# First shift and scale computed on TensorE in four column blocks, and the input projection summed block by block

## What is computed

```python
mod = jax.nn.silu(c) @ ada_w + ada_b              # (1, 1024) @ (1024, 6144)
sh_m, sc_m, g_m, sh_f, sc_f, g_f = jnp.split(mod, 6, axis=-1)
h = modulate(rms_norm(x, mix_norm_w), sh_m, sc_m) # xn * (1 + scale) + shift, (256, 1024)
proj = h @ w_in                                   # (1024, 3336)
y_r = rwkv7_group(proj[..., :1792], ...)          # chunks 0 to 6 of 256 columns
y_m = mlstm_group(proj[..., 1792:], ...)          # chunks 7 to 12, and 8 gate columns
```

## Time and profile before

| | us |
|---|---|
| median of 3 runs | 1258.65 |
| lowest, highest | 1250.43, 1260.34 |
| the profiled execution | 1263.12 |
| its span in the profile | 1261.0 |
| mean granted clock of TensorE over the span | 0.914 of full speed |

### The profile page before, as it was taken

How to read it: one execution, slowest core, us unless ns; L and a number is a source line. 1 busy time by engine, 2 the same in 40 slices (tenths; PEclk the granted TensorE clock), 3 DMA queues, 4 the chain that set the end, 5 groups by cost and what they waited for, 6 DMA issues and landing times.

```text
span 1261.0 us, 16196 instructions
## 1 busy us (share of the span) xinstructions
PE 1074.6 (85%) x6588; PEld 817.6 (65%) x6588; DVE 638.4 (51%) x812; ACT 351.5 (28%) x440; POOL 170.9 (14%) x224
## 2 busy tenths in 40 slices
PE   1699987999978889989639795979999976999994
PEld 1578853997535555555218674858888865888883
DVE  4556658546444323323046727375757467553433
ACT  0122014341111111111023104165445215543530
POOL 5400113000100133321020004011111130000000
PEclk9999967999977999999769896779999977999998
DMA  9897728204679999998979603057676461545510
GB/s 344 245 303 252 263 93 332 102 1 168 221 283 409 402 401 356 363 351 319 409 250 369 249 3 131 1 180 264 224 294 237 134 241 76 187 147 195 221 67 34
DMA packets 117162, 287.48 MB, mean 228 GB/s; under 512 B 19398, under 2 KB 45278, under 8 KB 117098
## 3 DMA queue, kind: packets, MB, share of 16 engines
q1 hardware_dynamic: 94514, 245.45, 52.1%
q10 hardware_dynamic: 11032, 27.33, 6.3%
q0 software_dynamic: 11552, 13.79, 3.6%
HBM read 334.23 MB, written 2.62 MB: 267 GB/s over the span
## 4 chain that ended last, share of the span: by engine, by line
PE 67%; DMA 14%; DVE 10%; SPq 3%; ACT 2%; ACTq 2%; issue 2%; POOL 1%; DVEq 0%; POOLq 0%
PE ps L573 29%; DMA arena<-in_moe_w_down_dram 6%; PE ps L2249 4%; PE ps L2584 4%; PE ps L2563 4%; PE ps L2423 3%; DMA ring<-in_w_in_dram 3%; DMA macc<-in_ada_w_dram 3%; PE ps L2611 3%; PE ps L2251 2%; PE ps L2510 2%; PE ps L2689 2%; SPq L763 1%; PE ps L1210 1%; SPq L619 1%
## 5 line engine op out<-in xcount | busy, mean ns | idle before, releaser
L578 DVE TENSOR_TENSOR ring_parts<-ring,arena_parts 128x2048 fp32r<-128x2048 f32 x65 | 146.6, 2285 | 49.8 <-ACT arena_parts L1098 43.2
L573 PE MATMUL ps<-arena_parts,macc_parts 128*128 128x512 f32 x512 | 165.9, 396 | 0.0
L573 PE MATMUL ps<-arena_parts,gate_parts 128*128 128x512 f32 x288 | 115.4, 401 | 8.0 <-DVE hT_parts L578 8.0
L573 PE MATMUL ps<-ring_parts,gate_parts 128*128 128x512 f32 x288 | 114.3, 397 | 0.0
L573 PE MATMUL ps<-arena_parts,hT_parts 128*128 128x512 f32 x288 | 114.2, 397 | 0.0
L573 PEld LDWEIGHTS ps<-arena_parts,macc_parts 128*128 128x128 f32 x512 | 96.2, 188 | 19.5
L573 PE MATMUL ps<-ring_parts,macc_parts 128*128 128x512 f32 x256 | 99.8, 390 | 0.0
L1098 ACT CAST arena_parts<-ring 128x2048 fp32r<-128x2048 f32 x32 | 60.4, 1908 | 86.2 <-DMA ring<-in_mlp_w_dram 44.1
L573 PEld LDWEIGHTS ps<-arena_parts,gate_parts 128*128 128x128 f32 x288 | 55.6, 193 | 20.3 <-DVE hT_parts L578 8.8
L2249 PE MATMUL ps<-hT,ring 128*128 128x256 f32 x288 | 68.0, 400 | 0.0
L2584 PE MATMUL ps<-ring,hT 128*32 128x256 f32 x1024 | 61.6, 394 | 4.2 <-DMA ring<-in_moe_w_gate_dram 2.7
(11 more groups left out here) (529 smaller groups left out, 1826.0 us busy)
## 6 DMA issues: line engine op xcount, KB each, us to landing
ring<-in_mlp_w_dram SPq DMA_DIRECT2D x40, 1024.0 KB, 7.6
arena<-in_moe_w_down_dram SPq DMA_DIRECT2D x16, 2048.0 KB, 12.3
ring<-in_ada_w_dram SPq DMA_DIRECT2D x29, 1024.0 KB, 9.0
ring<-in_mlp_w_dram ACTq DMA_DIRECT2D x24, 1024.0 KB, 7.1
ring<-in_moe_w_up_dram SPq DMA_DIRECT2D x10, 2048.0 KB, 18.5
ring<-in_moe_w_gate_dram SPq DMA_DIRECT2D x10, 2048.0 KB, 16.2
arena<-in_ada_w_dram SPq DMA_DIRECT2D x15, 1024.0 KB, 7.0
ring<-in_w_in_dram SPq DMA_DIRECT2D x13, 1024.0 KB, 12.3
```

Of the source, the lines that this page charges most:

```text
L573: ins = nc.tensor.matmul(o, l, r, start=start and i == 0, stop=stop and i == 2, skip_group_check=True)
L578: return eng.tensor_tensor(lo, x, hi.bitcast(F32), ALU.subtract)
```

## The change

- The matrices for shift and scale no longer go through DVE. They come as eight parts of 1 MB: for each block `b` of 256 output columns one part of shift and one of scale, 1024 x 256 each, in runs of 1 KB, into four homes of their own. SP issues them among the first chunks: parts 0 and 1, chunks 7 and 8, parts 2 and 3, chunks 9 and 10, parts 4 to 7, then chunk 11, ada 8, chunk 12, ada 9, ada 10, chunk 0, and so on. Parts 4 and 5 wait for the product of block 0, parts 6 and 7 for that of block 1.
- PE multiplies `c`, broadcast to 32 columns, by a part (16 products of 256 columns for a block, in four 32-row groups of the output), ACT copies the row out of PSUM, and four products of one column bring it into columns and sum the four groups. DVE adds the biases. DVE and ACT then scale one feature tile each in `hT`, in place; the plain transposed input has been copied there before.
- The four early chunks 7 to 10 have PSUM banks 6, 7, 2, 3 and are summed in pieces: after block `b` its two feature tiles are multiplied (chunks 9 and 10 join at block 1 with four tiles).
- Chunks 11 and 12 come directly after the gate columns, before the mLSTM products; before, they stood among them.
- The features are assigned to tiles in another order (`(t p)` where it was `(p t)`), so the transposes read without a stride.
- All small loads go from ACT to POOL. The product for the bias rows moves behind the gate columns on PE, and its copy and the write of `bias_rows` behind the gate activations on ACT.
- DVE uses ada slots 8 to 23 only; slot 9 moves from before the convolution to behind it.

The core of the diff:

```diff
-        stream = [("ada", n) for n in range(8)]
-        for i, n in enumerate(win_order):
-            stream += [("win", n)] + [("ada", 8 + i)]
-        stream += [("ada", n) for n in range(21, 24)]
+        win_early = win_order[:4]
+        stream = [("win", n) for n in win_early]
+        for n, adas in ((11, (8,)), (12, (9, 10)), (0, (11, 12)), (1, (13, 14)), (2, (15, 16)), (3, (17,)), (4, (18,)),
+                        (5, (19,)), (6, (20, 21, 22, 23))):
+            stream += [("win", n)] + [("ada", i) for i in adas]
...
             for i, (kind, n) in enumerate(stream):
+                if i in (0, 2):
+                    mix_part(i)
+                    mix_part(i + 1)
+                if i == 4:
+                    for j in range(4, 8):
+                        mix_part(j)
                 if i >= RING:
...
-            act.wait_ge(t_bias, 1)
-            nc.scalar.copy(ebc, ps[0:SWA_H, 4, 0:384]).then_inc(a_bias, 1)
-            act.wait_ge(a_bias, 1)
-            act.dma_start(scratch_d.rearrange("h (q l) -> h q l", q=P), ebc.unsqueeze(1).to_broadcast([SWA_H, P, 384])
-                          ).then_inc(bias_out, 16)
             act.wait_ge(x_in, 16)
-            a_norm(act, "n", mod_c[:, 0, :], mod_c[:, 1, :])
...
+            for b in range(4):
+                act.wait_ge(t["n"], STEP[f"n.rows{b}"])
+                c.link(nc.scalar.copy(mix_row, ps[:, 4, :]))
+                c.at(f"n.row{b}")
+                act.wait_ge(v["n"], STEP[f"n.mod{b}"])
+                c.link(nc.scalar.activation(hT[:, 2 * b, :], hT[:, 2 * b, :], ACT.Identity,
+                                            bias=mod_c[:, 0, 2 * b:2 * b + 1], scale=mod_c[:, 1, 2 * b:2 * b + 1]))
+                c.at(f"n.a{b}")
...
             cm.at("m.lf")
-            columns(9)
+            act.wait_ge(t_bias, 1)
+            nc.scalar.copy(ebc, ps[0:SWA_H, 4, 0:384]).then_inc(a_bias, 1)
+            act.wait_ge(a_bias, 1)
+            act.dma_start(scratch_d.rearrange("h (q l) -> h q l", q=P), ebc.unsqueeze(1).to_broadcast([SWA_H, P, 384])
+                          ).then_inc(bias_out, 16)
+            columns(11)
...
+            def mix_rows(b):
+                if b:
+                    pe.wait_ge(a["n"], STEP[f"n.row{b - 1}"])
+                for vec in range(2):
+                    j = 2 * b + vec
+                    pe.wait_ge(mix_in[j % 4], 16 * (j // 4 + 1))
+                    for k in range(KT):
+                        quad = slice(32 * (k % 4), 32 * (k % 4) + 32)
+                        ins = nc.tensor.matmul(ps[quad, 4, 256 * vec:256 * vec + 256], c1_b[:, k, :], mix_home[j % 4][:, k, :],
+                                               start=k < 4, stop=k >= 4, skip_group_check=True)
+                n_.mark(ins)
+                n_.at(f"n.rows{b}")
+                pe.wait_ge(a["n"], STEP[f"n.row{b}"])
+                pe.wait_ge(v["n"], STEP["n.mixc"] if b == 0 else STEP[f"n.mod{b - 1}"])
+                for i in range(4):
+                    ins = nc.tensor.matmul(ps[:, 5, 64 + i:65 + i], mix_row[:, P * i:P * i + P], quad_one, start=True, stop=True)
+                n_.mark(ins)
+                n_.at(f"n.cols{b}")
...
+            for b in range(4):
+                mix_rows(b)
+                for n in win_early[:2] if b < 2 else win_early:
+                    win_part(n, (2 * b, 2 * b + 1))
+                if b == 1:
+                    pe.wait_ge(prm_in, 16 * 14)
+                    nc.tensor.transpose(ps[:, 0, 256:312], prm[0:56, :], ident[0:56, 0:56])
+                    c.mark(nc.tensor.transpose(ps[:, 0, 312:408], prm2[0:96, :], ident[0:96, 0:96]))
+                    c.at("w.prm")
+                    for n in win_early[2:]:
+                        win_part(n, (0, 1, 2, 3))
```

More of the change, by code:

```diff
@@ L266, in program @@
         w_slot = small[:, 60:62]
+        quad_one = small[:, 62:63]
+        c1_b = macc[:, 1, 0:256].rearrange("p (k n) -> p k n", k=8)
+        mix_row = macc[:, 1, 256:768]
+        mix_home = [area(kb, SLOT).rearrange("p (t n) -> p t n", t=8) for kb in (0, 66, 22, 78)]
         third_gu = (0, 8, 40, 16)
@@ new lines, in _ @@
+            c = Counter(act, a["n"])
+            for tt in range(TT):
+                a_square(c, "n", tt)
+            for b in (1, 3):
+                act.wait_ge(t["n"], b + 1)
+                c.link(nc.scalar.copy(hT[:, 2 * b:2 * b + 2, :], ps[:, b, :].rearrange("p (k t) -> p k t", k=2)))
+                c.at(f"n.ev{b}")
+            for b in range(4):
[6 more added lines that the diff above has]
+                c.at(f"n.a{b}")
@@ L1306, in columns @@
                 c.at(f"w.col{n}")
-            for n in (7, 8):
+            for n in win_early:
                 columns(n)
@@ L1331, in _ @@
             cm.at("m.exp")
-            columns(12)
             for n in range(7):
@@ L1606, in _ @@
-            v_norm(dve, "n", mod_c[:, 0, :], mod_c[:, 1, :], mod_mix, meanwhile=lambda: ada_slot(6))
+            c.link(nc.vector.tensor_copy(c1_b, ccol[:, 0:8].unsqueeze(2).to_broadcast([P, 8, 32])))
+            dve.wait_ge(g["c"], STEP["c.ident"])
+            c.link(nc.vector.tensor_reduce(quad_one, ident[:, 0:P:32], AX_X, ALU.add))
+            c = Counter(dve, v["n"])
+            for tt in range(TT):
+                v_mean(dve, c, "n", tt)
+            for tt in range(TT):
+                v_xn(dve, c, "n", tt)
@@ new lines, in win_part @@
+            def win_part(n, ks):
+                loaded(pe, ("win", n))
+                pe.wait_ge(a["n"], STEP[f"n.a{ks[-1] // 2}"])
+                pe.wait_ge(v["n"], STEP[f"n.v{ks[-1] // 2}"])
+                w = slot(("win", n)).rearrange("p (t n) -> p t n", t=8)
+                for j in range(2):
+                    o = win_bank(n)[:, 256 * j:256 * j + 256]
+                    for k in ks:
+                        l, r = ((w[:, k, P * j:P * j + P], hT[:, k, :]) if n < 9 else (hT[:, k, P * j:P * j + P], w[:, k, :]))
+                        ins = nc.tensor.matmul(o, l, r, start=j == 0 and k == 0, stop=k == KT - 1, skip_group_check=True)
+                if ks[-1] == KT - 1:
+                    ins.then_inc(t_win, 1)
@@ L2267, in _ @@
             c.at("w.if")
-            for n in (9, 10):
+            pe.wait_ge(hot_in, 32)
+            nc.tensor.matmul(ps[0:SWA_H, 4, 0:384], rel_sb[0:33, :], hots[0:33, :], start=True, stop=True).then_inc(t_bias, 1)
+            for n in (11, 12):
                 columns(n)
@@ L2283, in _ @@
             m.at("m.sc0")
-            columns(11)
+            columns(0)
             pe.wait_ge(v["m"], STEP["m.z"])
@@ L2288, in _ @@
             m.at("m.sc1")
-            columns(12)
-            columns(0)
+            columns(1)
+            columns(2)
             pe.wait_ge(v["m"], STEP["m.pt"])
@@ L2302, in _ @@
             m.at("m.num")
-            for n in range(1, 6):
+            for n in range(3, 6):
                 columns(n)
```

148 lines of the change are left out of this document (82 added, 66 removed), and 7 rows, old and new, of the table STEP.

## The result

The changed kernel is slower: a median of 1266.87 us against 1258.4 for the kernel before beside it, 20 runs each, a ratio of 1.0079 with a 95% interval of 1.0055 to 1.0102. The medians lie 8.5 us apart, and the ratio is worth 9.9 (7 to 13), where 3 less were forecast: the sign was wrong. That 1266.87 lies within the forecast range of 1243 to 1268 says little, as the range holds both signs. One run of the changed kernel took 3722.39 us; the ratio leaves it out, and the median without it is 1266.42. The profiled execution took 1268.72 us (before 1263.12), its span is 1267.0, the mean granted clock 0.912 (0.914).

The account below looks back on a forecast made before the run. Loads bound the kernel up to 49.85 us, PE afterwards. E 70.7 plus 96.9 put chunk 6's end at 167.6 against 170.65, 3 us less: 1260.1 for the profiled execution, 1255.7 for the median, range 1243 to 1268.

Parts of the forecast that it names:

- packet for packet: Bias write beside ring loads: each engine alternates their packets, so a chunk's load takes 15.4 us, an ada slot's 3.8.
- a stall of 8 us: PE before chunk 2, behind the early chunks: waits 8 us for its load, held up by the bias write.
- the price of a lull: PE's clock after the short chains of blocks 1 to 3: 0 to 2 us each, taken as 1.
- Block plan and loads: First stage: 3.6 us a load, last part at 50; block 1's last row products 29.6; no load waits from block 2.
- The 45 by the Trainium skill's rule of line rate: First-stage loads: if 1 KB runs cost nothing, the last lands at 45 and the stage ends some 3 us sooner.
- E: End of early chunks 7 to 10 on PE, before the gate columns: forecast 70.7 us, low 64.7, high 76.
- The rival of the clock: First stage: PE's clock stays down in the pieces, E 87, chunk 6 at 184, 13 us more, 1272; chance 0.13.
- the sum behind E: PE work from gate columns through chunks 0 and 1: chunk 2 due at E + 36, only 0.7 us added.
- The write: Bias rows on ACT's queue behind the gate activations: eight engines, E + 10.5 to E + 40.5, chunk 2 landing at E + 44.
- Cold start: PE after the stall before chunk 2: the lower clock adds 1 us.
- From there on: Chunk 2 to chunk 6: DVE's shifts and slots nearly late, last column sum and chunk 6 taken as 9 us.
- The sum to chunk 6: End of chunk 6 on PE: E + 96.9 = 167.6 against 170.65 before, 3 us less.

Follow-up runs that it names:

- e3: Changed kernel with dummy products filling the PE lulls of blocks 1 to 3; median 1262.26 us, ratio 1.0028 to the kernel before.
- e6: Changed kernel with the bias-row write issued behind ACT's copy of chunk 11, 3 to 4 us later, still 8 partitions; 1264.19 us, ratio 1.0065.
- e7: Changed kernel with the bias-row write from 16 partitions and dummy products in the lulls of blocks 1 to 3; 1252.39 us, ratio 0.9962.
- the second pair of profiles: Both kernels profiled once more, unchanged; profiled executions 1262.96 us (changed) and 1259.06 us (before).
- e4: Changed kernel with the bias rows held twice and written from 16 partitions instead of 8, in the same place; 1255.05 us, ratio 0.9968.
- e8: Changed kernel with the 16-partition write and dummy products in the lulls of blocks 0 to 3; 1252.22 us, ratio 0.9975.
- e1: Changed kernel with the whole bias work, write included, moved behind the input projection (write at 217 us); 1259.36 us, ratio 0.9980.
- e5: Kernel before with the bias rows written from 16 partitions in their old place; 1258.38 us, ratio 1.0019.
- e9: Changed kernel with the bias work early again (write at 29 us, 8 partitions); 1272.63 us, ratio 1.0113.
- e2: Kernel before with the whole bias work, write included, moved to about 225 us; 1253.66 us, ratio 0.9959.
- e11: Changed kernel once more, unchanged, for a second profile; profiled execution 1262.96 us.

## Why the prediction was wrong, step by step

Two steps failed. The larger is the exchange "packet for packet" between the write and the loads from the write's first packet on: it gave chunk 1 in time and a stall of 8 us, and the runs show a load issued behind the write shut out of its engines for about 15 us, a stall of 10.9 and 1.9 of restart. The other is the price of a lull, taken as 1 us and measured as 2.8, 1.7 and 1.7.

- **Block plan and loads: right.** Block 1's last row products end at 27.52, not 29.6, and the last part, issued at about 39 and 12.0 us in flight, lands near 51 (50 forecast). That the mean of 3.6 us a load came out is in part luck: the last parts, in runs of 1 KB, land 3.0 us apart (47.70 and 50.71), and between 20 and 38 us GpSimd's loads bring 1.73 MB that the sum had only as a surcharge. The 45 by the Trainium skill's rule of line rate (DMA: Bandwidth & Descriptors, Specifications) is not what the trace shows. Of the rule itself: the ada slots behind the parts, in runs of 4 KB, land 2.5 to 2.7 us behind the load before them (56.35 and 61.73), so runs of 1 KB do cost some 0.4 us a load. Blocks 2 and 3 waited for no load.
- **Lulls: the mechanism right, the size wrong.** The row behind it was the earlier trace rows: 2 us. I took 1 each, "0 to 2", and measured 2.8, 1.7 and 1.7 (e3). That is 3.2 more than in the sum, and the chains of the blocks took 0.9 more than reckoned; E came out at 72.65 instead of 70.7 only because the loads gave back 2 us. The rival of the clock (0.13) was half true: 6 us lost, not 16. By its own line, more than 6 us of dense work at the low level undo the 3 us gained, and so they would have here without the loads. The same shows a dip at chunk 0, which the sum behind E left out. It is there again (8.86), in six of the thirteen profiles and not in the others: 1.5 to 1.7 us by chance.
- **The write: right in engines, start, rate and length, wrong in what it does to the loads.** E + 10.5 forecast for its packets and E + 10.2 measured (82.8), 31 us, eight engines. "Packet for packet" was read from 63 to 68 us of before, the last third of the write. In its second half it holds in the changed kernel too; the first half had its engines to itself, 83 to 98 us. So chunk 1, held to be in time at E + 28, landed at E + 41.9, and the stall is 10.9 us before chunk 1, not 8 before chunk 2. e6 put chunk 1 ahead of the write and had the same stall before chunk 2. The kernel before had shown it: its write was issued at 31.79 (row below), the next chunk at 34.40, and one for one from the write's start near 40 on, 64 packets in 15.4 us, would have landed that chunk near 55 (an estimate from the earlier trace rows). It landed at 70.85, 36.45 us after its issue, the very row that the prediction set beside its 15.4 and passed over, since PE had waited for it only 1.4 us.

```profile
31.79 0.81 ACTq L1278 DMA_DIRECT2D bias_rows<-arena  x1
```

- **Cold start: 1 us taken, 1.9 measured** (15.98 against 14.08).
- **From there on: right.** From the end of chunk 5 to that of chunk 6 18.6 us, 18.9 forecast. The sum let PE stand until DVE is done; in the trace PE is busy until 0.71 us before that with the first column sums (1.88 and 3.73), which the sum left out. DVE does end last, so the time is the same. As its work starts behind the numerators, it moves with PE: the wait is 0.71 in e7 too.

The sum to chunk 6 was 167.6 and should have been 175.2. The 7.6 between are, to 0.1, the terms above: E 2.0, the dip 1.7, the stall 2.9 and the restart 0.9. Against before that is 4.5 later instead of 3 earlier. The median shows 8.5 later. The other 4 us (2 with the second pair of profiles) are not found. The profiled executions themselves differ by 5.6 us in the first pair (1268.72 and 1263.12) and 3.9 in the second (1262.96 and 1259.06), about what chunk 6 shows. For each of after, e3, e4, e6, e7 and e8 the median stands 2 to 7 us worse against before than chunk 6 does, for e1 10; but for e5, a form of the kernel before, it does so too (3.7), for e9 it doesn't, and the profiles show no stage behind chunk 6 that is longer in all of them. Stretches at which PE's clock is high in some executions and low in others (780 to 806, 292 to 296) are the likely place; that they fall worse for the changed kernel is argued, not shown.

What the change was made for came true in good part: the early chunks and the gate columns end at 76.2 instead of 84.9, 8.7 us ahead where 10.5 were forecast. The write took more than that back behind them (10.9 and 1.9), and less than half of what it had cost in the kernel before was seen beforehand (1.4 of some 3.7 us, e2).

## What to carry to other kernels

Before a large DMA is moved, look at how many of the 16 engines it uses (packets per microsecond over the rate of one engine), and widen its outermost size first: here 16 rows instead of 8 turned a loss of 8.5 us into a gain of 3. A write on half of the engines beside loads on all of them holds up each load issued behind it (30 us instead of 5 here), since a load is complete only with its slowest engine; ask what is queued ahead of the write and what behind. And a rate of exchange read in one stretch of a transfer is to be held against the flight time of a whole load beside it: here 15.4 us by the rate stood next to 36.45 in the trace. Where a dense stage is cut into blocks with short serial chains between, count each lull at the clock's price that the trace shows, or fill it with dummy products (three lulls filled here: E 3.7 us earlier with a slow block 0 in that profile, 6.2 us of clock).

## What the hardware showed that was not expected

- The write keeps its engines from loads issued behind it for a while: eight engines for 15 us in after, all sixteen in e4 for its whole length of 15.5 us (82.8 to 98.4), and only then was the exchange one for one. In after, e3 and e11 it ends with 504 of the write's packets sent, about 63 an engine, in e6, where loads queued ahead still ran, with 574. Why it ends there is open, and so is whether the held-up packets wait in the queue of the engine or are not yet handed to it.
- SP's issue instruction itself takes long when the loads ahead don't drain: 14.62 us from the start of the first of two to the end of the second in after (about 2 of it a wait between them), 40.81 for four in e9, against 0.37 for one into a free queue. Loads behind it are late before they are even queued.
- PE's clock falls or doesn't in the same place of the same program: block 0's pieces took 3.69 us (after) or 6.48 (e11), chunk 0 7.17 or 8.86, and the stretch at 780 to 806 us differs by 5 to 7 us.
